# Feed-forward down projections with seven block products per pair of chunks instead of eight

## Chip, cores, metric

One core of one Trainium2 chip runs the whole program. Times are microseconds of device time, the median of 3 runs. TensorE (PE) multiplies, VectorE (DVE), ScalarE (ACT) and GpSimd (POOL) work element by element, SyncE (SP) issues most of the loads. All data are fp32.

## What is computed

The reference is a model of three blocks on 256 tokens of width 1024. Two layers of the first kind each have two feed-forwards around a mixer (a state-space scan, then neighbourhood attention) and end in a gated side input; a third layer of another kind follows, with three attention branches and a squared-ReLU MLP. What the change touches are the four feed-forwards:

```
D_MODEL = 1024; SEQ = 256; D_FF = 2816
def swiglu(x, w_gu, w_down):
    g, u = jnp.split(x @ w_gu, 2, axis=-1)
    return (jax.nn.silu(g) * u) @ w_down
for i in range(DEPTH):                      # 2 layers
    h = h + 0.5 * swiglu(rmsnorm(h, ffn1_norm[i]), ffn1_w_gu[i], ffn1_w_down[i])
    ...                                     # the mixer
    h = h + 0.5 * swiglu(rmsnorm(h, ffn2_norm[i]), ffn2_w_gu[i], ffn2_w_down[i])
    ...                                     # the gated side input
```

A down projection multiplies 256 x 2816 by 2816 x 1024.

## The kernel before

**Products.** Every fp32 product is made of three matmuls in the fp32r type: both operands are split into a rounded part ("hi") and the residue ("lo"), and hi*hi, hi*lo and lo*hi are added up in PSUM. For weights the hi part is a ScalarE copy from `raw` to `whi`, the lo part a VectorE subtraction `wlo = raw - whi` (the function `ahead` of each engine, the operations themselves in the helpers `copy`, L1412, and `tt`, L1967).

**The stream of weight tiles.** `plan_of` (L156) lists all 284 tiles of the program in their order, each up to 128 x 2048 elements, 1 MB. SyncE loads them in this order into four slots (`NRAW`), each load waiting until the slot's earlier tile is split. ScalarE and VectorE split tiles into three slots (`NSPL`). `take(label)` on each of the two marks the place where a tile is used, and first splits ahead: the tile two after it. ScalarE's split waits for the load and until TensorE has released the tile three before it. TensorE waits for both parts (`take`, L574) and signals `w_rel` when it has used them. So the order of all work on an engine is the order in which its program calls `take` and the steps between.

**A feed-forward** (`ffn` in each engine's program). The up stage has 11 steps `c`, each with two tiles, 48 matmuls of 512 columns: the first 256 columns are gate, the second 256 are up. ScalarE makes the SiLU into `ftmp`, VectorE the product into `fa`, 128 tokens x 256 features for each of two token halves `t`. One step later, TensorE transposes it (`turn_a`) into PSUM bank 4 or 5, and `high_a` (ScalarE) and `low_a` (VectorE) split it into `aThi` and `aTlo`: 22 chunks of 128 features x 256 tokens, the stationary operand of the down projection.

The down stage (`down`, L724) goes over column halves `c` of 512 columns and in each over 6 tiles of four chunks (the last one of two). For each chunk and token half, three matmuls of 512 columns add to a PSUM bank: banks 6 and 7 for the first half of the columns, 2 and 3 for the second. That is 22 x 2 x 2 x 3 = 264 matmuls. VectorE adds 0.5 x bank to `h` (`residual`), the next stage's transposes (`turn`), squares and splits (`early_quarters`, `late_quarters`) are placed between the tiles of the second half and behind it.

**GpSimd** takes the inverse square roots of the norms (one-column powers, `rstds`), some sums in the state-space mixer (gate<-gate), the bias sums of the neighbourhood attention (bm<-tb,cst) and two residues in the third layer. It is idle in feed-forwards but for the roots. The bias table `tb` is loaded by `table` in SyncE's program.

Of the kernel before, what the change touches and what calls it, by code (L numbers as in the profile page):

```python
# [18 lines left out]
TILE = 2048  # L19

# [23 lines left out]
def constants():  # L44
# [30 lines left out]
    "a_weigh": "exps", "v_outputs": "yev yg yTlo", "a_outputs": "yThi ysq",  # L75
# [69 lines left out]
class Plan:  # L145


    def __init__(self):
        self.tiles, self.index = [], {}

    def add(self, label, pieces, a, b):
        self.index[label] = len(self.tiles)
        self.tiles.append((pieces, a, b))


def plan_of(dr):  # L156
    p = Plan()

    def ffn(i, up, down, extra=None):
# [64 lines left out]
PREP = (8, 16, 24)  # L224
HALVES = 2 * len(PREP) + 2
# [129 lines left out]
def programs(dr, mem, banks, plan, ev):  # L355
# [11 lines left out]
    pool_tiles = set()  # L367

    def wview(name, n):
        _, a, b = plan.tiles[n]  # L370
        slots = NRAW if name == "raw" else NSPL
        return mem[name][:, n % slots, 0:a * b].rearrange("p (a b) -> p a b", a=a)

    def wflat(name, n, slots):
        _, a, b = plan.tiles[n]
        return mem[name][:, n % slots, 0:a * b]
# [117 lines left out]
    def sync(S):  # L494
# [3 lines left out]
        def load(n):  # L498
            pieces, a, b = plan.tiles[n]
            slot = wflat("raw", n, NRAW).rearrange("p (a b) -> p a b", a=a)  # L500
            if n >= NRAW:
                last = (n - NRAW,) if n - NRAW > 1 else (n - NRAW, 3)
                S.wait_ge(*at("w_hi", *last))
                S.wait_ge(*at("w_lo" if n - NRAW not in pool_tiles else "w_lo_p", *last))
            c = 0
            for src in pieces:
                wd = src.shape[2]
                e.dma_start(slot[:, :, c:c + wd], src).then_inc(*sig(f"d_w{n % NRAW}", n, by=16))
# [8 lines left out]
        def table():  # L517
            rp = dr["rpb"]
            S.wait_ge(*at("h", 4, 1, 1))
# [23 lines left out]
        for n in range(2, len(plan.tiles)):  # L543
# [4 lines left out]
            if n == tile["down", 2, 0, 0]:  # L548
                pos(1)
# [10 lines left out]
    def tensor(T):  # L560
# [13 lines left out]
        def take(*label):  # L574
# [5 lines left out]
            T.wait_ge(*at("w_lo_p" if n in pool_tiles else "w_lo", n))  # L580
# [115 lines left out]
        def closing_block(labels, bs, xhi, xlo, first, between=None):  # L696
# [6 lines left out]
            for t in range(2):  # L703
                for i, (label, hi, lo, kk) in enumerate(held):
                    nk = hi.shape[1]
                    for k in range(nk):
# [4 lines left out]
                        if between and t and i == 0 and k == 1:  # L711
                            between()
# [11 lines left out]
        def down(name, xhi, xlo, tiles, r, turn_last):  # L724

            for c in range(2):
                bs = ACC[c]
                clear(*bs)
                for y in range(tiles - 2):
# [3 lines left out]
                    if y == 0:  # L733
                        if c == 0:
                            turn_last()
                        elif r < 10:
                            turn(r, 0, 0)
                            turn(r, 1, 0)
# [2074 lines left out]
```

## Time and profile before

| | |
|---|---|
| median of 3 runs | 1678.13 us (1677.65 to 1678.68) |
| span of the profiled execution | 1676.1 us |
| TensorE busy | 1664.8 us (99%) |
| VectorE busy | 1068.0 us (64%) |
| ScalarE busy | 898.6 us (54%) |
| GpSimd busy | 86.1 us (5%) |
| weight residues wlo on VectorE | 284, 622.4 us |
| weight hi parts on ScalarE | 284, 518.2 us |
| bytes moved | 300.58 MB, mean 179 GB/s |

The profiled execution's span is 2.0 us under the median of the runs: the span is counted from the first to the last instruction. Busy time of TensorE is the union of its matmuls, whose ends are modelled; the time that one matmul costs is read from start to start. The rows that the prediction rests on stand below.

### The profile page before, as it was taken

The page shows a single profiled execution, that of the slowest core. Times are in us where ns is not written, and L with a number is a line of the kernel's source. Part 1 is how long each engine was busy: PE and PEld are TensorE (multiplying, and loading weights), DVE is VectorE, ACT ScalarE, POOL GpSimd, SP SyncE. Part 2 cuts the span into 40 slices and gives each one's busy share as a digit, 9 for nine tenths or more (in the row PEclk, how much of TensorE's full clock was granted, in tenths as well). Part 3 has the DMA queues.
Part 4 walks back from the last instruction along what each step waited for, and adds up shares of the span by engine and source line. Part 5 has one row for each costly group of instructions (what it writes and reads, how often), then busy time and mean ns, then how long its engine had stood idle before and what let it go on. Part 6 is the DMA issues. An engine that isn't in the chain of part 4 may idle for free.

```text
span 1676.1 us, 23021 instructions
## 1 busy us (share of the span) xinstructions
PE 1664.8 (99%) x9366; PEld 1426.7 (85%) x9366; DVE 1068.0 (64%) x1364; ACT 898.6 (54%) x1279; POOL 86.1 (5%) x79
## 2 busy tenths in 40 slices
PE   8999999999999999999999999999999999999998
PEld 6888899999788888888888778888889999988886
DVE  5554678999965545755457766555655577766643
ACT  5443566777864444744346665444553556564532
POOL 0000000000100000000007500000000000000000
PEclk9999999999999999999999999999999999999999
DMA  9655567666466554686555336655565533465551
GB/s 306 192 178 184 158 191 208 179 196 209 156 200 198 187 188 165 188 242 209 181 175 195 119 101 214 185 180 188 180 197 153 174 103 126 152 211 178 176 192 60
DMA packets 243978, 300.58 MB, mean 179 GB/s; under 512 B 9248, under 2 KB 175520, under 8 KB 243872
## 3 DMA queue, kind: packets, MB, share of 16 engines
q1 hardware_dynamic: 238224, 289.25, 54.5%
q10 hardware_dynamic: 5648, 9.85, 2.2%
q8 instruction: 75, 1.23, 0.3%
q14 instruction: 31, 0.25, 0.0%
HBM read 297.96 MB, written 1.11 MB: 178 GB/s over the span
## 4 chain that ended last, share of the span: by engine, by line
PE 99%; DVE 1%; DMA 0%; ACT 0%; ACTq 0%; DVEq 0%; issue 0%
PE bank L564 95%; PE bank L567 4%; DMA h<-in_x 0%; DVE wlo L1967 0%; DVE hTlo L1970 0%; DVE xn L1970 0%; DVE h L1970 0%; ACT hThi L1412 0%; DVE xn L2019 0%; DVEq L2740 0%; ACT xn L1409 0%; ACTq L1924 0%; ACTq L1923 0%; ACT L1920 0%; ACTq L2740 0%
## 5 line engine op out<-in xcount | busy, mean ns | idle before, releaser
L1967 DVE TENSOR_TENSOR wlo<-raw,whi 128x2048 fp32r<-128x2048 f32 (+2 forms) x284 | 622.4, 2195 | 326.5 <-ACT whi L1412 326.5
L1412 ACT ACTIVATE whi<-raw 128x2048 fp32r<-128x2048 f32 (+2 forms) x284 | 518.2, 1832 | 244.8 <-PE bank L564 240.9
L564 PE MATMUL bank<-whi,hThi 128*128 128x512 f32 x1056 | 420.7, 398 | 0.0
L564 PE MATMUL bank<-wlo,hThi 128*128 128x512 f32 x1056 | 412.3, 390 | 0.3 <-DVE wlo L1967 0.3
L564 PE MATMUL bank<-whi,hTlo 128*128 128x512 f32 x1056 | 396.8, 391 | 0.0
L564 PE MATMUL bank<-hThi,whi 128*128 128x256 f32 x888 | 253.3, 285 | 0.0
L564 PE MATMUL bank<-hThi,wlo 128*128 128x256 f32 x888 | 251.2, 283 | 0.0
L564 PE MATMUL bank<-hTlo,whi 128*128 128x256 f32 x888 | 251.2, 283 | 0.0
L564 PEld LDWEIGHTS bank<-whi,hThi 128*128 128x128 f32 x1056 | 198.6, 188 | 44.3 <-issue 6.0
L564 PEld LDWEIGHTS bank<-whi,hTlo 128*128 128x128 f32 x1056 | 198.5, 188 | 42.6 <-DVE hTlo L1970 0.3
L564 PEld LDWEIGHTS bank<-wlo,hThi 128*128 128x128 f32 x1056 | 198.8, 188 | 40.5 <-DVE wlo L1967 1.8
L564 PEld LDWEIGHTS bank<-hThi,whi 128*128 128x128 f32 x888 | 169.5, 191 | 3.6 <-issue 3.1
L564 PEld LDWEIGHTS bank<-hThi,wlo 128*128 128x128 f32 x888 | 169.5, 191 | 0.2
L564 PEld LDWEIGHTS bank<-hTlo,whi 128*128 128x128 f32 x888 | 169.5, 191 | 0.2
L564 PE MATMUL bank<-whi,aThi 128*128 128x512 f32 x352 | 137.8, 391 | 0.0
L564 PE MATMUL bank<-whi,aTlo 128*128 128x512 f32 x352 | 137.1, 389 | 0.0
L564 PE MATMUL bank<-wlo,aThi 128*128 128x512 f32 x352 | 137.0, 389 | 0.0
L1412 ACT ACTIVATE aThi<-bank 128x512 fp32r<-128x512 f32 x44 | 26.3, 598 | 155.1 <-PE bank L567 155.1
L1409 ACT ACTIVATE ftmp<-bank,st 128x256 f32<-128x256 f32 x88 | 41.5, 475 | 105.6 <-PE bank L564 105.5
L2564 POOL TENSOR_TENSOR st<-st,cst 128x1 f32<-128x1 f32 (+2 forms) x35 | 36.5, 1057 | 1147.4 <-DVE st L1992 1075.2
L1967 DVE TENSOR_TENSOR aTlo<-bank,aThi 128x512 fp32r<-128x512 f32 x44 | 30.4, 691 | 80.8 <-ACT aThi L1412 80.8
L564 PEld LDWEIGHTS bank<-whi,aTlo 128*128 128x128 f32 x352 | 66.1, 188 | 13.8
(222 smaller groups left out, 1883.4 us busy)
## 6 DMA issues: line engine op xcount, KB each, us to landing
raw<-in_ffn_w_gu SPq DMA_DIRECT2D x172, 512.0 KB, 4.9
raw<-in_ffn_w_down SPq DMA_DIRECT2D x40, 1024.0 KB, 5.0
raw<-in_w_in SPq DMA_DIRECT2D x30, 1024.0 KB, 5.2
raw<-in_ssd_w_in SPq DMA_DIRECT2D x16, 1024.0 KB, 5.6
raw<-in_ssd_w_in SPq DMA_DIRECT2D x32, 512.0 KB, 5.5
raw<-in_w_up SPq DMA_DIRECT2D x16, 1024.0 KB, 5.4
raw<-in_w_down SPq DMA_DIRECT2D x16, 1024.0 KB, 5.0
raw<-in_na_w_qkv SPq DMA_DIRECT2D x12, 1024.0 KB, 5.2
```

Of the source, the lines that this page charges most:

```text
L564: return T.e.matmul(out, lhsT, rhs, start=start, stop=stop, skip_group_check=skip)
L567: return T.e.transpose(out, in_, ident)
L1409: return e.activation(out, in_, func, **kw)
L1412: return e.activation(out, in_, ACT.Identity, **kw)
L1967: return e.tensor_tensor(out, a, b, op)
L2564: return e.tensor_tensor(out, a, b, op)
```

## The change

For 14 of the 22 chunks, in 7 pairs, the 2 x 2 block matrix of activations (two token halves x two chunks) is multiplied with the 2 x 2 block matrix of weights (two chunks x two column halves) with seven block products in place of eight, after Strassen and Winograd. Write A11, A21 for the two token halves of the pair's first chunk, A12, A22 for those of the second, and B11, B12 (first chunk), B21, B22 (second chunk) for the column halves of the weights.

- **Weights.** A `paired` tile is a load of 2 chunks x 1024 columns, in the order B12, B11, B22, B21. Its last 1536 columns are split. A `mixed` tile is not loaded: it is the four sums B11+B12, B12+B22, B11+B12+B22, B11+B12+B22+B21, made by GpSimd (1024 columns in one operation, then 512) and VectorE (the last 512) in one of three buffers `ts0` to `ts2`, and then split like any tile, 2048 columns. `ts1` and `ts2` lie where the normalised input of the up stage was, `ts0` on the buffers of the differences.
- **Activations.** ScalarE copies the transposes of the first 7 steps also into `araw`; GpSimd makes the differences `dsum`, in operations of 256, 128 and 128 columns (`differences`); ScalarE and VectorE split them (`high_d`, `low_d`) one step later. In place of A21 split directly at the place of the second token half, `aThi` holds there what the seven products need.
- **Order of the down stage** (`mixed_down` in three engines' programs): a tile of four chunks of the first column half (chunks 14 to 17), the last transposes, pair 0, pair 1, a tile of two chunks of the second half, pairs 2 to 6, then the last four chunks of the first half and the last six of the second. A pair is 9 matmuls with the paired tile and 12 with the mixed one.
- **Merge.** The seven products go to all eight banks; products shared by several blocks are added at the end by six VectorE operations, one ScalarE copy and two GpSimd sums of 512 columns (`merged`), before the residuals.
- `table` waits for the last mixed tile of the third feed-forward and is issued before a tile of the attention; the GpSimd path for weight residues (`pool_tiles`, empty) goes; in GpSimd's program the roots, pair sums and merges are put in the order of the stages.

The core of the diff:

```diff
+PAIRS = 7
...
+REST = {(0, 0): (14, 4), (0, 1): (18, 4), (1, 0): (14, 2), (1, 1): (16, 4), (1, 2): (20, 2)}
...
-        for c in range(2):
-            for y in range(6):
-                nk = min(4, 22 - 4 * y)
-                p.add(("down", i, c, y), [wsrc(down, 4 * y, nk, c * 512, 512)], nk, 512)
+        rest(0, 0)
+        for j in range(PAIRS):
+            p.add(("paired", i, j), [wsrc(down, 2 * j, 2, 512, 512), wsrc(down, 2 * j, 2, 0, 512)], 2, 1024)
+            p.add(("mixed", i, j), None, 4, 512)
+            if j == 1:
+                rest(1, 0)
+        rest(0, 1)
+        rest(1, 1)
+        rest(1, 2)
...
 SyncE, load(n)
                 S.wait_ge(*at("w_hi", *last))
-                S.wait_ge(*at("w_lo" if n - NRAW not in pool_tiles else "w_lo_p", *last))
+                S.wait_ge(*at("w_lo", *last))
+                if labels[m][0] == "paired":
+                    S.wait_ge(*at("tsum", *labels[m][1:]))
...
 SyncE, table
-            S.wait_ge(*at("h", 4, 1, 1))
+            S.wait_ge(*at("w_rel", "mixed", 2, PAIRS - 1))
...
-            if n == tile["up", 2, 0, 0] + 8:
+            if n == tile["qkv", NA_CHUNKS[1], 0]:
                 table()
...
 TensorE
+            def seven(j):
+                first, final = j == 0, j == PAIRS - 1
+                hi, lo = take("paired", i, j)
+                T.wait_ge(*at("aTlo", i, j))
+                T.wait_ge(*at("dTlo", i, j))
+                three_products(0, block_of(2 * j, 0), hi[:, 0, 512:1024], lo[:, 0, 512:1024], first, final)
+                three_products(2, difference(j, 2), hi[:, 1, 0:512], lo[:, 1, 0:512], first, False)
+                three_products(6, block_of(2 * j + 1, 0), hi[:, 1, 512:1024], lo[:, 1, 512:1024], False, False).then_inc(
+                    *sig("w_rel", "paired", i, j))
+                hi, lo = take("mixed", i, j)
+                if first:
+                    clear(4)
+                three_products(4, difference(j, 0), hi[:, 0, :], lo[:, 0, :], first, final)
+                three_products(5, block_of(2 * j, 1), hi[:, 1, :], lo[:, 1, :], first, final)
+                three_products(1, difference(j, 1), hi[:, 2, :], lo[:, 2, :], first, final)
+                three_products(7, block_of(2 * j + 1, 1), hi[:, 3, :], lo[:, 3, :], False, False).then_inc(*sig("w_rel", "mixed", i, j))
...
+            clear(6, 7)
+            rest(0, 0, (6, 7), (True, True))
+            turn_last()
+            clear(0, 1, 2, 3, 5)
+            for j in range(PAIRS):
+                seven(j)
+                if j == 1:
+                    rest(1, 0, (2, 3), (False, True))
...
+            closing_block([("down", i, 0, 1)], (6, 7), aThi, aTlo, REST[0, 1][0])
+            residual_in(r, 0, (6, 7))
+            held, k0 = [], REST[1, 1][0]
+            for y in (1, 2):
+                hi, lo = take("down", i, 1, y)
+                held += [(hi[:, k, :], lo[:, k, :], y) for k in range(REST[1, y][1])]
...
 ScalarE, high_a
+                if c >= 2:
+                    A.wait_ge(*at("dsum", i, c - 2))
+                copy(mem["araw"][:, c % 2, :], b).then_inc(*sig("araw", i, c))
+                copy(aThi[:, 2 * c, 0:P], b[:, 0:P])
+                copy(aThi[:, 2 * c + 1, :], b[:, 256:512]).then_inc(*sig("aThi", i, c))
+
+            def high_d(c):
+
+                A.wait_ge(*at("dsum", i, c))
+                d = mem["dsum"][:, c % 2, :]
+                copy(aThi[:, 2 * c, P:256], d[:, 0:P])
+                copy(flat(mem["dThi"][:, c, :, :]), d[:, P:512]).then_inc(*sig("dThi", i, c))
...
 VectorE, ahead
+                if labels[n][0] == "paired":
+                    w, o = mem["raw"][:, plan.raw_of[n] % NRAW, :], mem[f"ts{labels[n][2] % 3}"][:, :]
+                    V.wait_ge(*at("tsecond", *labels[n][1:]))
+                    tt(o[:, 1536:2048], o[:, 1024:1536], w[:, 1536:2048], ALU.add).then_inc(*sig("tsum", *labels[n][1:]))
                 V.wait_ge(*at("w_hi", n))
...
 VectorE
+            def low_d(c):
+
+                V.wait_ge(*at("dThi", i, c))
+                d = mem["dsum"][:, c % 2, :]
+                tt(aTlo[:, 2 * c, P:256], d[:, 0:P], f(aThi[:, 2 * c, P:256]), ALU.subtract)
+                tt(flat(dTlo(c)), d[:, P:512], f(flat(mem["dThi"][:, c, :, :])), ALU.subtract).then_inc(*sig("dTlo", i, c))
+
+            def merged():
+
+                um, wm = flat(mem["ftmp"][:, :, :]), flat(fa[:, :, :])
+                V.wait_ge(*at("root", i))
+                stt(h[:, 0, chunk(0)], banks[0], 0.5, h[:, 0, chunk(0)], ALU.mult, ALU.add).then_inc(*sig("h11", i))
+                V.wait_ge(*at("w_rel", "mixed", i, PAIRS - 1))
+                stt(um, banks[1], 0.5, um, ALU.mult, ALU.subtract).then_inc(*sig("um", i))
+                stt(h[:, 0, chunk(1)], banks[4], 0.5, h[:, 0, chunk(1)], ALU.mult, ALU.add).then_inc(*sig("h12p", i))
+                V.wait_ge(*at("um", i))
+                stt(wm, banks[5], 0.5, um, ALU.mult, ALU.add).then_inc(*sig("wm", i))
+                stt(h[:, 1, chunk(1)], banks[4], 0.5, h[:, 1, chunk(1)], ALU.mult, ALU.add).then_inc(*sig("h22p", i))
+                V.wait_ge(*at("wm", i))
+                tt(h[:, 1, chunk(0)], h[:, 1, chunk(0)], wm, ALU.subtract).then_inc(*sig("h21", i))
+
+            def mixed_down(r):
+                take("down", i, 0, 0)
+                low_a(10)
+                for j in range(PAIRS):
+                    take("paired", i, j)
+                    take("mixed", i, j)
+                    if j == 1:
+                        take("down", i, 1, 0)
+                merged()
+                take("down", i, 0, 1)
+                V.wait_ge(*at("h21", i))
+                for t in range(2):
+                    residual(r, t, 0, half(("down", i, 0, 1), t), 6 + t, 0.5)
+                take("down", i, 1, 1)
+                early_quarters(r)
+                V.wait_ge(*at("h22", i))
...
 GpSimd
+        def sums(i, j):
+
+            n = tile["paired", i, j]
+            w, o = mem["raw"][:, plan.raw_of[n] % NRAW, :], mem[f"ts{j % 3}"][:, :]
+            halves = lambda x: x.rearrange("p (x c) -> p x c", x=2)
+            G.wait_ge(*landed(n))
+            if j >= 3:
+                G.wait_ge(*at("w_lo", tile["mixed", i, j - 3]))
+            elif j:
+                G.wait_ge(*at("w_rel", "up", i, 10, 1))
+            else:
+                G.wait_ge(*at("dTlo", i, PAIRS - 1))
+            tt(halves(o[:, 0:1024]), halves(w[:, 512:1536]), w[:, 0:512].unsqueeze(1).to_broadcast([P, 2, 512]), ALU.add).then_inc(*sig("tfirst", i, j))
+            G.wait_ge(*at("tfirst", i, j))
+            tt(o[:, 1024:1536], o[:, 0:512], w[:, 1024:1536], ALU.add).then_inc(*sig("tsecond", i, j))
+
+        def ffn(i, extra=None):
+            for c in range(PAIRS):
+                differences(i, c)
+                if c == 2 and extra is not None:
+                    ple_rstd(extra)
+            for j in range(PAIRS):
+                sums(i, j)
+            G.wait_ge(*at("h12p", i))
+            tt(h[:, 0, chunk(1)], h[:, 0, chunk(1)], flat(mem["ftmp"][:, :, :]), ALU.add).then_inc(*sig("h12", i))
+            G.wait_ge(*at("wm", i))
+            G.wait_ge(*at("h22p", i))
+            tt(h[:, 1, chunk(1)], h[:, 1, chunk(1)], flat(mem["fa"][:, :, :]), ALU.add).then_inc(*sig("h22", i))
```

## Rows read from the trace of the kernel before

**Rows 1.** The page, part 1: engine, busy us, share of the span, instructions.

```profile
PE 1664.8 (99%) x9366; PEld 1426.7 (85%) x9366; DVE 1068.0 (64%) x1364; ACT 898.6 (54%) x1279; POOL 86.1 (5%) x79
```

**Rows 2.** Waits of TensorE: total us, times, longest.

```profile
PE bank L567 <- DMA h<-in_x: 2.8, 2, 2.5
PE bank L564 <- DVE fa L2532: 1.2, 1, 1.2
PE bank L564 <- DVE wlo L1967: 0.3, 1, 0.3
```

**Rows 3.** Order of time on TensorE: start us, us of the instruction, operation.

```profile
136.94 0.39 PE L564 MATMUL bank<-whi,aThi 128*128 128x512 f32 x1
...
139.66 0.39 PE L564 MATMUL bank<-whi,aThi 128*128 128x512 f32 x1
```

**Rows 4.** Groups by shape, ScalarE and VectorE: busy us, mean ns, idle before.

```profile
L1412 ACT ACTIVATE whi<-raw 128x2048 fp32r<-128x2048 f32 x262 | 500.1, 1913 | 208.4 <-PE bank L564 204.5 <-DMA cum<-ct 3.2 <-DMA raw<-in_ffn_w_gu 0.7
L1412 ACT ACTIVATE whi<-raw 128x1024 fp32r<-128x1024 f32 x12 | 12.7, 1057 | 28.2 <-PE bank L564 28.2
L1967 DVE TENSOR_TENSOR wlo<-raw,whi 128x1024 fp32r<-128x1024 f32 x12 | 14.7, 1223 | 18.8 <-ACT whi L1412 18.8
```

**Rows 5.** The page, part 6: KB of one load, us from issue to landing.

```profile
raw<-in_ffn_w_down SPq DMA_DIRECT2D x40, 1024.0 KB, 5.0
```

**Rows 6.** Order of time on VectorE, back-to-back operations.

```profile
416.62 0.68 DVE L1967 TENSOR_TENSOR EW<-Er,cst 128x512 f32<-128x512 f32 x1
417.22 0.68 DVE L1967 TENSOR_TENSOR Er<-Er,later 128x512 f32<-128x512 f32 x1
...
449.73 2.28 DVE L1967 TENSOR_TENSOR wlo<-raw,whi 128x2048 fp32r<-128x2048 f32 x1
451.93 3.54 DVE L1967 TENSOR_TENSOR EW<-EW,bank 128x1024 f32<-128x1024 f32 x4
```

**Rows 7.** Order of time on GpSimd; x12 is a run of twelve.

```profile
453.31 1.30 POOL L2564 TENSOR_TENSOR gate<-gate 128x512 f32<-128x512 f32 x1 [9.14 <-DVE EW L1967]
458.58 3.21 POOL L2564 TENSOR_TENSOR gate<-gate 128x512 f32<-128x512 f32 x1 [3.97 <-ACT gate L1409]
...
895.95 7.29 POOL L2564 TENSOR_TENSOR bm<-tb,cst 128x256 f32<-128x256 f32 x8
...
906.39 14.15 POOL L2564 TENSOR_TENSOR bm<-tb,cst 128x256 f32<-128x256 f32 x12
...
1027.98 0.54 POOL L2564 TENSOR_TENSOR st<-st,cst 128x1 f32<-128x1 f32 x1 [22.14 <-DVE st L2105]
1028.70 2.52 POOL L2564 TENSOR_TENSOR st<-st,cst 128x1 f32<-128x1 f32 x1 [0.18 <-DVE st L2105]
...
1375.95 3.14 POOL L2564 TENSOR_TENSOR oS<-oT,oS 128x1024 fp32r<-128x1024 f32 x1 [156.57 <-ACT oS L1412]
```

**Rows 8.** Order of time on VectorE, residues beside the GpSimd operations of rows 7.

```profile
458.35 2.28 DVE L1967 TENSOR_TENSOR wlo<-raw,whi 128x2048 fp32r<-128x2048 f32 x1
...
896.68 2.75 DVE L1967 TENSOR_TENSOR wlo<-raw,whi 128x2048 fp32r<-128x2048 f32 x1
...
907.15 5.46 DVE L1967 TENSOR_TENSOR wlo<-raw,whi 128x2048 fp32r<-128x2048 f32 x2
...
915.04 2.85 DVE L1967 TENSOR_TENSOR wlo<-raw,whi 128x2048 fp32r<-128x2048 f32 x1
...
1028.55 2.28 DVE L1967 TENSOR_TENSOR wlo<-raw,whi 128x2048 fp32r<-128x2048 f32 x1
...
1374.56 2.29 DVE L1967 TENSOR_TENSOR wlo<-raw,whi 128x2048 fp32r<-128x2048 f32 x1 [1.06 <-ACT whi L1412]
```

**Rows 9.** Order of time on VectorE, two residual additions in a feed-forward.

```profile
170.39 1.28 DVE L1970 SCALAR_TENSOR_TENSOR h<-bank,h 128x512 f32<-128x512 f32 x2
```

**Rows 10.** Stretches of an up stage: busy us of each engine, clock, DMA.

```profile
30.00:100.00 70.00, 70.00 (x322) 57.90 (x321) 37.78 (x33) 32.72 (x31) 0.00 (x0) 1.00 0.65 204
```

**Rows 11.** The same view at the opening; PEclk 1.00 is full speed.

```profile
5.00:10.00 5.00, 2.39 (x10) 1.63 (x10) 1.61 (x5) 2.26 (x8) 0.00 (x0) 0.80 1.02 350
```

More of the change, by code:

```diff
@@ L542, in sync @@
         e.dma_start(cst[:, 130:NCST], dr["cst"][:, 130:NCST]).then_inc(*sig("d_c2", by=16))
-        for n in range(2, len(plan.tiles)):
+        for n in plan.raws[2:]:
             if n == tile["yout", 7] + 5:
                 pos(0)
-            if n == tile["up", 2, 0, 0] + 8:
+            if n == tile["qkv", NA_CHUNKS[1], 0]:
                 table()
-            if n == tile["down", 2, 0, 0]:
                 pos(1)
@@ L579, in take @@
             T.wait_ge(*at("w_hi", n))
[L580 removed]
+            T.wait_ge(*at("w_lo", n))
             return wview("whi", n), wview("wlo", n)
@@ L735, in down @@
                             turn_last()
[L736 to L740 removed]
+                closing_block([name + (c, tiles - 2), name + (c, tiles - 1)], bs, xhi, xlo, 4 * (tiles - 2))
                 residual_in(r, c, bs)
@@ new lines, in mixed_down @@
+            def mixed_down(r):
+                take("down", i, 0, 0)
+                low_a(10)
+                for j in range(PAIRS):
+                    take("paired", i, j)
+                    take("mixed", i, j)
+                    if j == 1:
+                        take("down", i, 1, 0)
+                merged()
+                take("down", i, 0, 1)
+                V.wait_ge(*at("h21", i))
+                for t in range(2):
+                    residual(r, t, 0, half(("down", i, 0, 1), t), 6 + t, 0.5)
+                take("down", i, 1, 1)
+                early_quarters(r)
+                V.wait_ge(*at("h22", i))
+                for t in range(2):
+                    residual(r, t, 1, half(("down", i, 1, 2), t), 2 + t, 0.5)
+                    if r == 1 and t == 0:
+                        low(1, 0, 1)
+                        mean_square(1, 0)
+                if r == 1:
+                    scaled(0)
+                take("down", i, 1, 2)
+                if r == 1:
+                    mean_square(1, 1)
+                    low(1, 1, 1)
+                    scaled(1)
+                else:
+                    late_quarters(r)
@@ L2564, in tt @@
             return e.tensor_tensor(out, a, b, op)
-        def ahead(m):
-            while G.ready < min(m, len(plan.tiles)):
-                n = G.ready
-                G.ready += 1
-                if n in pool_tiles:
-                    G.wait_ge(*at("w_hi", n))
-                    tt(wflat("wlo", n, NSPL), wflat("raw", n, NRAW), f(wflat("whi", n, NSPL)), ALU.subtract).then_inc(*sig("w_lo_p", n))
-        def take(*label):
-            ahead(tile[label] + NSPL)
         def rstds(r):
@@ L2637, in three @@
             for what, n in three_steps():
-                if what == "gate" and n % 2 == 0:
-                    take("gate", n // 2)
-                elif what == "keep" and n in (3, 7):
+                if what == "keep" and n in (3, 7):
                     br = n // 4
```

198 lines of the change are left out of this document (135 added, 63 removed).

## The prediction

> **What bounds the kernel now.** I read the page from its totals downward: TensorE is busy for 1664.8 of 1676.1 us [rows 1]. The modelled ends of the matmuls could make that share look too good, so the second view is who waited for whom: TensorE waited 4.3 us in the whole execution, only 0.3 us of it for a weight split [rows 2]. So nothing but the number of matmuls sets the time, and a microsecond of them removed anywhere is a microsecond of span, as long as the other engines still deliver ahead of TensorE. Third, the order of time on TensorE at the start of a down projection: from 136.94 to 139.66 lie twelve equal steps, 2.72 / 12 = 0.2267 us from start to start; the 0.39 us of one is its latency, which overlaps the next [rows 3].
>
> **What the change removes.** A pair of 128-row chunks against both column halves and both token halves is eight block products of three matmuls, 24; now it is seven, 21. That is 3 x 7 pairs x 4 feed-forwards = 84 matmuls of 512 columns, 84 x 0.2267 = 19.0 us; a down projection goes from 264 matmuls to 243. The weights' bytes stay the same. With nothing else, the time would be 1678.1 - 19.0 = 1659.1 us (the profiled span is 1676.1; what lies around it is the difference to the median of the runs, 2.0 us, and I leave it as it is).
>
> **What it adds, per pair.** ScalarE: splits of 1536 and 2048 columns in place of one of 2048. At 1.91 us for 2048 and 1.06 for 1024 [rows 4] that is 1.5 + 1.9 = 3.4 us, against a pair's TensorE time of 21 x 0.2267 = 4.76 us: hidden. DMA: one 1 MB load per pair, 5.0 us to landing, asked for at least a pair ahead: hidden [rows 5].
>
> VectorE: the residues of 1536 and 2048 columns and one sum of 512. A 2048-column residue holds VectorE for 2.20 us (449.73 to 451.93 [rows 6]), one of 1024 for about 1.14 (its 1.22 [rows 4] less the same overlap), so one of 1536 for about 1.67; a two-input SBUF operation of 512 takes 0.60 to the next (416.62 to 417.22 [rows 6]). Sum 2.20 + 1.67 + 0.60 = 4.47 us, still under 4.76.
>
> GpSimd: a sum of 1024 columns and one of 512. A free 512-column sum takes 1.30 us, some 1.2 of it without its start-up; 1024 columns took 3.14 us, of which the first 0.90 lay under a VectorE residue, so 2.24 free (1375.95 in [rows 7], 1374.56 in [rows 8]). Sum 2.24 + 1.2 = 3.44 us, also under 4.76.
>
> **Where I see the cost: the two do not run side by side.** [Rows 7] and [rows 8] have to be laid over each other. The 512-column GpSimd sum takes 1.30 us at 453.31 and 3.21 us at 458.58. In the second case VectorE's residue wlo<-raw,whi runs from 458.35 to 460.63, and the sum ends at 461.79, 1.16 us later: it did its whole work afterwards. A one-column power takes 0.54 us free and 2.52 us at 1028.70; the residue beside it ends at 1030.83, the power 0.39 us after that. The reverse also happens: the residue at 896.68 took 2.75 us instead of 2.29, with GpSimd in a run of eight bias sums, 7.29 us with that residue inside. Taking its 2.20 out leaves 0.64 for one. Twelve of them from 906.39 lie beside three residues, two from 907.15 and one at 915.04: 12 x 0.64 + 3 x 2.20 = 14.3, and the row has 14.15. By contrast the sum at 453.31, beside VectorE operations with one operand in PSUM (EW<-EW,bank from 451.93 [rows 6]), was not delayed. So in this kernel VectorE with two SBUF inputs and GpSimd exclude each other for a whole instruction, in turns.
>
> The Trainium skill states this as a rule that speaks against the change (SBUF — State Buffer, section "SBUF: two separate sides"): the port pair that both engines share is an exclusive lock held for the instruction, and a VectorE operation with two SBUF inputs takes it against a GpSimd operation that reads SBUF. By that rule, the trace agrees, the sum comes out as below; without it, as in rival A.
>
> All the new work is of that kind: residues, sum, GpSimd sums. A pair needs 4.47 + 3.44 = 7.9 us of a resource for which TensorE leaves it 4.76.
>
> **How much of that reaches the end.** Let time 0 be where TensorE finishes the last up tile; before it GpSimd can do only the first pair's sums, since the other two sum buffers lie on the up stage's inputs. The last mixed tile can be multiplied once its residue is done, which needs, after time 0: on VectorE seven mixed residues, 7 x 2.20 = 15.4, six paired ones, 6 x 1.67 = 10.0, six sums, 3.6, and the residue of the two-chunk tile, 1.14, together 30.2; on GpSimd six pairs' sums, 6 x 3.44 = 20.6. Sum 50.8 us. TensorE would be there after 24 matmuls, 5.4, the last transposes, 0.4 (an estimate: under two matmuls' worth for four narrow ones), six pairs, 28.6, nine matmuls, 2.0, and the two-chunk tile, 2.7: 39.1 us. It is late by 11.7 us. Stepping through in turns I find no long time when both are idle, and VectorE never waits for ScalarE, since a pair that takes 7.9 us leaves its 3.4 free. Four feed-forwards: 46.8 us.
>
> Bounds: if start-up that queued instructions hide takes 0.2 us off each GpSimd operation (12) and 0.1 off each VectorE one (20), the sum is 46.4 and the lateness 7.3 (four times, 29); if each of some 32 turns costs 0.1 us and the 1024-column sum takes the whole 3.14 us of its row, it is 50.8 + 3.2 + 5.4 = 59.4, 20.3 us late (four times, 81). I take 11.7, since the run of 14.15 us fits turns without a price.
>
> **The end of the down projection.** After it starts the last mixed tile (2.7) TensorE has a four-chunk tile (5.4) before it needs the residue of the last two-chunk tile. From the same moment VectorE has two residues of 2.20, six merges of 512 columns at about 0.64 (two h sums take 1.28 [rows 9]) and that residue, 1.14: 9.4 us, and 1.2 more if a GpSimd sum of the merge is in front. TensorE waits 1.3 to 2.5 us, less what VectorE is ahead; I take 1.5, four times 6 us, between 0 and 12. The residuals that follow are due 2.0 us later and take 1.3: hidden.
>
> **At nothing.** In the up stage GpSimd's differences (512 columns a chunk in three operations, some 1.5 us), the extra ScalarE copies (about 1.3 us) and the extra small residues (0.6 us) lie in a block of 48 matmuls, 10.9 us, of which VectorE is busy for little over half (37.78 of 70 us [rows 10]). A residue behind a difference waits 0.7 us and is due half a block, 5.4 us, later. Without that cover it would be 0.7 us x 28 = 20 us. The bias table's load waits for the third feed-forward's last mixed tile, 15 us before the stage ends; the loads queued behind it on SP are for tiles later than the closing ones, and its users start in the attention. GpSimd's new order puts the norm roots where their inputs come anyway.
>
> **Sum.** 1678.1 - 19.0 + 46.8 + 6.0 = 1711.9, so 1712 us.
>
> **The rivals.**
> A, the other side, faster: the exclusion is not what these rows show, for instance because sums with a repeated operand read differently, and GpSimd's sums slip beside the residues. Then VectorE needs 4.47 and GpSimd 3.44 of 4.76 us, each in time, and the merge remains: 1659.1 + 6 = 1665 us. The change gains once the lateness is under (19.0 - 6.0) / 4 = 3.25 us, so once 8.4 of the 20.6 us of GpSimd's sums slip. Against it: every overlap that I found, in both directions, has the delay. Chance 0.10.
> B, half: 4 to 8 us of the sums slip, lateness about 6 us: 1659.1 + 24 + 6 = 1689 us. For it: no row shows how much of an instruction's own start-up lies outside the exclusion, and queued ones may hide it. Chance 0.14.
> C, worse: turns have a price, or the wide sum takes 3.14: up to 1659.1 + 81 + 6 = 1746 us. A second way there: TensorE idling 3 us in 8 could lower its clock. The profile shows 0.80 between 5 and 10 us [rows 11], after the sparse opening, and full clock ever after; with TensorE working 60% of the time I expect full clock. Chance 0.12.
> D, no effect: gain and loss cancel, lateness near 3.25 us. 0.02.
>
> **How the numbers follow.** Forecast 0.62 (1698 to 1730), B 0.14, C 0.12, A 0.10, D 0.02. A measurement here tells about 0.2%, 3.4 us, from no change. Faster: A and a little of B, 0.11; same: D, 0.02; slower: the rest, 0.87. Range 1684 to 1736: it takes in most of B and the lower half of C and leaves A out.
>
> **What would show it.** In the order of time of a down projection: VectorE and GpSimd working in turns, GpSimd's 1024-column sums at 2.2 us free and up to 4.5 with a residue in front, 2048-column residues at up to 4.4 instead of 2.29. TensorE waiting for wlo, some 45 us in total, in mixed and paired tiles from the second pair on, and 1 to 2 us for the last wlo of each feed-forward. No gaps in up stages, clock full. The prediction is wrong if residues beside GpSimd sums stay at 2.29 us and the sums at 2.2 and 1.3 (then A); if they are undisturbed and TensorE waits anyway, the waits name another place.

## The result and the profile after

| | before | changed |
|---|---|---|
| median | 1677.89 us (1677.38 to 1678.68, 4 runs) | 1724.85 us (1720.34 to 1726.17, 4 runs) |
| ratio to before | | 1.0274, 95% interval 1.0260 to 1.0289 |
| span of the profiled execution | 1676.1 us | 1718.5 us |

The change makes the kernel 2.7% slower. The forecast was slower, 1712 us, range 1684 to 1736. The profiled execution of the changed kernel is the lowest of its four runs (1720.34); the others have spans of 1722.2 to 1724.4, so the median lies some 4.5 us above what the trace below can account for.

The page of the changed kernel, the parts that answer to [rows 1]: busy us, share and instructions of each engine, then the engines' shares of the chain of work that ended last.

```profile
PE 1663.9 (97%) x9282; PEld 1413.2 (82%) x9282; DVE 1229.2 (72%) x1528; ACT 971.0 (57%) x1423; POOL 290.1 (17%) x227
...
PE 87%; DVE 11%; ACT 1%; DMA 0%; issue 0%; DVEq 0%; ACTq 0%
```

84 matmuls are gone (9366 to 9282), the span is longer. The chain that ended last, second line, now has VectorE for 11%. The waits of TensorE, answering to [rows 2] (total us, times, longest):

```profile
PE bank L602 <- DVE wlo L2103: 26.3, 17, 2.3
PE bank L602 <- issue: 11.5, 10, 1.5
PE bank L602 <- ACT whi L1520: 6.1, 6, 2.0
```

The residues that TensorE waited 0.3 us for now cost it 26.3 us. The next two lines name something else, but in the down stages each of these waits, too, ends 0.10 us after the end of a weight residue on VectorE, so they are waits for the same tiles. But for 0.6 us of the opening and the first up stage, all of it lies in the down stages. From the first to the last matmul of each down projection it was 61.5, 61.0, 61.0 and 61.0 us before and 73.8, 71.2, 71.3 and 71.3 us after, together 43.0 us more; the three stretches between them and the one behind the last changed by less than 0.1 us, the opening by 0.4. The second of them as one stretch, before and then after (length, busy us of PE, PEld, DVE, ACT, POOL, clock, DMA share, GB/s):

```profile
604.60:665.60 61.00, 61.00 (x277) 50.62 (x276) 28.02 (x24) 24.28 (x26) 0.00 (x0) 1.00 0.53 182
```

```profile
616.50:687.70 71.20, 60.42 (x256) 46.91 (x255) 63.55 (x43) 35.96 (x34) 35.43 (x14) 0.98 0.51 170
```

VectorE goes from 28 busy us of 61 to 63.6 of 71.2, much of it not work but waiting inside the instruction. That is seen when its order of time is laid beside GpSimd's, as [rows 7] and [rows 8] were. The first down projection, VectorE:

```profile
145.34 2.85 DVE L2103 TENSOR_TENSOR wlo<-raw,whi 128x1536 fp32r<-128x1536 f32 x1
148.11 4.49 DVE L2103 TENSOR_TENSOR wlo<-ts,whi 128x2048 fp32r<-128x2048 f32 x1
152.52 2.29 DVE L2103 TENSOR_TENSOR wlo<-raw,whi 128x1024 fp32r<-128x1024 f32 x1
154.74 2.88 DVE L2103 TENSOR_TENSOR ts<-ts,raw 128x512 f32<-128x512 f32 x1
...
178.66 1.75 DVE L2103 TENSOR_TENSOR wlo<-raw,whi 128x1536 fp32r<-128x1536 f32 x1
...
185.60 2.29 DVE L2103 TENSOR_TENSOR wlo<-ts,whi 128x2048 fp32r<-128x2048 f32 x1 [0.32 <-ACT whi L1520]
```

and GpSimd in the same stretch:

```profile
136.80 2.41 POOL L2746 TENSOR_TENSOR ts<-raw 128x1024 f32<-128x1024 f32 x1 [14.60 <-PE bank L602]
...
144.95 1.62 POOL L2746 TENSOR_TENSOR ts<-ts,raw 128x512 f32<-128x512 f32 x1
146.54 3.91 POOL L2746 TENSOR_TENSOR ts<-raw 128x1024 f32<-128x1024 f32 x1
150.53 3.21 POOL L2746 TENSOR_TENSOR ts<-ts,raw 128x512 f32<-128x512 f32 x1
153.70 3.37 POOL L2746 TENSOR_TENSOR ts<-raw 128x1024 f32<-128x1024 f32 x1
...
173.30 2.69 POOL L2746 TENSOR_TENSOR ts<-ts,raw 128x512 f32<-128x512 f32 x1
```

Read the ends. GpSimd ends at 146.57, 150.45, 153.74; in between VectorE gets its turn and ends at 148.19 and 152.60. A residue of 2048 columns that takes 2.29 us free takes 4.49, one of 1024 columns 2.29 (free 1.22), a sum of 512 columns 2.88 (free 0.69). After 176 us GpSimd has finished, and VectorE's rows are back at 1.75 and 2.29 us.

### The profile page after: what moved, and what is told of

It is laid out like the page before. It is cut to its first block, busy times and chain, and to the rows that moved or that the text cites. A ratio compares the mean times of both kernels' runs of the same rounds, so it can differ in the third digit from the quotient of the medians.

```text
span 1718.5 us, 23453 instructions
## 1 busy us (share of the span) xinstructions
PE 1663.9 (97%) x9282; PEld 1413.2 (82%) x9282; DVE 1229.2 (72%) x1528; ACT 971.0 (57%) x1423; POOL 290.1 (17%) x227
## 4 chain that ended last, share of the span: by engine, by line
PE 87%; DVE 11%; ACT 1%; DMA 0%; issue 0%; DVEq 0%; ACTq 0%
PE bank L602 83%; DVE wlo L2103 8%; PE bank L605 4%; DVE ts L2103 1%; ACT whi L1520 0%; DVE h L2106 0%; DMA prm<-in_prm 0%; DVE h L2103 0%; DVE aTlo L2103 0%; ACT aThi L1520 0%; DVE ftmp L2106 0%; DVE fa L2106 0%; ACT hThi L1520 0%; DVE rTlo L2106 0%; DVE hTlo L2106 0%
## 5 line engine op out<-in xcount | busy, mean ns | idle before, releaser
L2103 DVE TENSOR_TENSOR wlo<-raw,whi 128x2048 fp32r<-128x2048 f32 (+2 forms) x284 | 641.2, 2263 | 208.0 <-ACT whi L1520 207.6
L1520 ACT ACTIVATE whi<-raw 128x2048 fp32r<-128x2048 f32 (+2 forms) x284 | 507.3, 1792 | 164.7 <-PE bank L602 161.2
L602 PE MATMUL bank<-whi,aThi 128*128 128x512 f32 x240 | 98.2, 409 | 26.6 <-issue 11.5
L2746 POOL TENSOR_TENSOR ts<-raw 128x1024 f32<-128x1024 f32 x28 | 79.9, 2853 | 158.5 <-DMA raw<-in_ffn_w_down 75.1
L602 PE MATMUL bank<-whi,aTlo 128*128 128x512 f32 x240 | 95.5, 398 | 0.0
L602 PE MATMUL bank<-wlo,aThi 128*128 128x512 f32 x240 | 95.3, 397 | 0.0
L1520 ACT ACTIVATE whi<-ts 128x2048 fp32r<-128x2048 f32 x28 | 53.7, 1918 | 64.1 <-DVE ts L2103 61.6
L2103 DVE TENSOR_TENSOR wlo<-ts,whi 128x2048 fp32r<-128x2048 f32 x28 | 81.8, 2920 | 7.8 <-ACT whi L1520 7.8
```

Source lines behind the costliest of these rows:

```text
L602: return T.e.matmul(out, lhsT, rhs, start=start, stop=stop, skip_group_check=skip)
L1520: return e.activation(out, in_, ACT.Identity, **kw)
L2103: return e.tensor_tensor(out, a, b, op)
L2746: return e.tensor_tensor(out, a, b, op)
```

## The experiments

Times are medians, ratios against the kernel before run on the same chip in the same call.

**GpSimd writes, but reads nothing.** Weight sums left out, constant fills of the same columns in their place.

```diff
-            tt(halves(o[:, 0:1024]), halves(w[:, 512:1536]), w[:, 0:512].unsqueeze(1).to_broadcast([P, 2, 512]), ALU.add).then_inc(*sig("tfirst", i, j))
+            e.memset(o[:, 0:1024], 0.5).then_inc(*sig("tfirst", i, j))
...
-            tt(o[:, 1024:1536], o[:, 0:512], w[:, 1024:1536], ALU.add).then_inc(*sig("tsecond", i, j))
+            e.memset(o[:, 1024:1536], 0.5).then_inc(*sig("tsecond", i, j))
```

> Leaves out the weight sums of GpSimd: in their place it fills the same 1024 and 512 columns with a constant, in the same place of its program and behind the same semaphores, so it writes but reads nothing. Theory P (VectorE with two SBUF inputs and GpSimd reading SBUF exclude each other): GpSimd takes no turns from VectorE any more, the 2048-column residues of mixed tiles fall from 2.92 us mean to 2.29, the 1536-column ones from 2.70 to 1.76, TensorE waits only at the merge (4 x 2.4 us) and at full clock: 1659 + 10 = 1669 us, 1664 to 1675. Rival W (they exclude each other whatever GpSimd does): fills of perhaps a third of the sums' time still block, 1685 to 1700. Rival V (VectorE is bound by its own added work, not by turns): its work is unchanged, 1718 to 1728.

Measured 1675.44 us (1671.86 to 1677.56), ratio 0.9984 (0.9975 to 0.9993): VectorE's own added work is all still there, and the time is 49 us below the changed kernel's. It is 0.4 us over the range expected, and the granted clock goes with that: the five runs at 0.998 took 1671.9 to 1674.6 us, the five at 0.994 to 0.996 took 1676.3 to 1677.6. Rival V (VectorE bound by its own work) is out. The groups by shape (busy us, mean ns, idle before), first the changed kernel's:

```profile
L2103 DVE TENSOR_TENSOR wlo<-ts,whi 128x2048 fp32r<-128x2048 f32 x28 | 81.8, 2920 | 7.8 <-ACT whi L1520 7.8
L2103 DVE TENSOR_TENSOR wlo<-raw,whi 128x1536 fp32r<-128x1536 f32 x28 | 75.5, 2695 | 0.4
```

then this one's:

```profile
L2103 DVE TENSOR_TENSOR wlo<-ts,whi 128x2048 fp32r<-128x2048 f32 x28 | 64.2, 2293 | 17.3 <-ACT whi L1520 17.3
L2103 DVE TENSOR_TENSOR wlo<-raw,whi 128x1536 fp32r<-128x1536 f32 x28 | 49.1, 1755 | 1.9 <-ACT whi L1520 1.2
```

Both residues are back at their free duration. The fills are shorter than the sums (0.96 and 0.53 us), so this alone does not say that they don't exclude VectorE. Two rows where they overlap do, GpSimd and VectorE of this kernel:

```profile
157.57 0.96 POOL L2841 MEMSET ts<- 128x1024 f32 x1 [3.59 <-DVE wlo L2103]
158.59 0.53 POOL L2843 MEMSET ts<- 128x512 f32 x1
...
157.97 1.75 DVE L2103 TENSOR_TENSOR wlo<-raw,whi 128x1536 fp32r<-128x1536 f32 x1
```

Neither is prolonged. The exclusion needs a GpSimd operation that reads; rival W is out.

**The last sum back on GpSimd.**

```diff
 VectorE, ahead
-                    tt(o[:, 1536:2048], o[:, 1024:1536], w[:, 1536:2048], ALU.add).then_inc(*sig("tsum", *labels[n][1:]))
 GpSimd, sums
+            G.wait_ge(*at("tsecond", i, j))
+            tt(o[:, 1536:2048], o[:, 1024:1536], w[:, 1536:2048], ALU.add).then_inc(*sig("tsum", i, j))
```

> Undoes one part: the last weight sum (512 columns) of each pair goes back to GpSimd. Theory P: GpSimd gets 1.24 us more a pair and VectorE 0.60 less, the sum grows by 0.64 x 6 = 3.8 us a feed-forward: 1724.9 + 15 = 1740 us, 1732 to 1748. Rival V: VectorE is relieved of 0.60 x 6 x 4 = 14 us: 1711 us. Rival L (GpSimd works ahead and only the hand-overs count): about as now, 1720 to 1730.

Measured 1738.03 us (1736.95 to 1739.47), ratio 1.0358 (1.0342 to 1.0373): 13 us slower than the changed kernel. Work taken off the busier engine made it slower, because the other one holds the shared resource twice as long for it. Of the three readings on record only the sum over both engines has that sign. It is not the whole of it: the last mixed residue now ends 56.3 us after the first down matmul, 4.9 later than in the changed kernel where 3.8 was expected, since VectorE stands idle three times for 3.1 us in each stage, waiting for GpSimd's sums and ScalarE's copy of them; part of that comes back at the end of the stage.

**The residue in front of the merge.**

```diff
-                merged()
                 take("down", i, 0, 1)
+                merged()
                 V.wait_ge(*at("h21", i))
```

> VectorE's residue of the last two-chunk tile is placed before the six merges instead of behind them. The gap of 2.7 us from start to start at the last block of each feed-forward (2.4 us lost) goes; the merges come 1.1 us later and the transposes of the next stage, due 2.0 us into the block, may wait about 0.5 us: 1724.9 - 4 x 1.9 = 1717 us, 1713 to 1721. If the gap is not the residue's but the merges' (banks or h), no change, 1722 to 1727.

Measured 1709.28 us (1708.70 to 1709.83), ratio 1.0187 (1.0170 to 1.0204). That is 15.6 us below the changed kernel, twice what was expected. The gap of 2.7 us from start to start is gone and nothing takes its place in three of four stages (68.8 us against 71.2). The first takes 69.8 against 73.8: there a stretch at half clock (granted clock 0.5, some 1.4 us lost) lay in the closing block, and it is gone as well. The stages together give 11.4 us, and 0.3 lies in the opening. Most of the rest comes from the profiled runs: the changed kernel's lies 4.5 us under its median, this one's 0.6. So the merge order was worth 2.4 us a stage, not 1.5, and in the first stage the half clock on top of it.

**All sums on VectorE**, each in front of the residue of its paired tile.

```diff
 VectorE, ahead, of a paired tile
-                    V.wait_ge(*at("tsecond", *labels[n][1:]))
+                    V.wait_ge(*landed(n))
+                    ...  # the two sums of GpSimd's sums(i, j), then the third
 GpSimd, ffn
-            for j in range(PAIRS):
-                sums(i, j)
```

> All three weight sums (1024, 512, 512 columns) on VectorE, none on GpSimd. Theory P: a 512-column sum costs the shared resource 0.60 us on VectorE and 1.2 on GpSimd, so a pair needs 2.20 + 1.67 + 1.14 + 0.60 + 0.60 = 6.2 us of it instead of 7.9; after time 0 that is 15.4 + 10.0 + 1.1 + 6 x 2.34 = 40.6 us against TensorE's 39.1: 1.5 us late, with some 0.3 us a pair of waiting for whi about 3. Time 1659 + 4 x (3 + 2.4) = 1681 us, 1673 to 1692, the half-clock windows mostly gone. Rival V (VectorE's own time bounds): 1.74 us more per pair on VectorE on top of today's lateness, 6 x 1.74 x 4 = 42 us more: 1766 us. Rival L (the hand-over GpSimd, VectorE, ScalarE, VectorE is what costs): one hand-over less, 1700 to 1715.

Measured 1713.65 us (1712.50 to 1714.85), ratio 1.0212 (1.0197 to 1.0227). Faster than the changed kernel by 11 us, but 33 us off the expectation. Rival V is out again, but the time lies in the range of rival L, so this run alone does not decide between L and the sum. The trace has free durations for the sums and for the paired and mixed residues, and each pair takes 6.86 us on VectorE, from start to start 1.25 and 1.34 for the sums, 1.75 for the paired residue, a wait of 0.31 for ScalarE's whi and 2.21. Lateness had been summed as if VectorE worked from time 0; it stood still for some 3 us before the last aTlo, and the first sum, in line behind it, began 7.3 us after time 0.

**Seven pairs, the same sums ahead.** Sums of pair 1 right after the up stage, of pair 2 before aTlo, of pair j + 1 between the two residues of pair j; four-chunk tiles for the two-chunk ones.

```diff
 VectorE, after the residue of tile n
+                if labels[n][0] == "paired" and 3 <= labels[n][2] + 1 < PAIRS:
+                    vsum(labels[n][1], labels[n][2] + 1)
 VectorE, mixed_down
+                vsum(i, 1)
                 take("down", i, 0, 0)
+                vsum(i, 2)
                 low_a(10)
```

> Seven pairs, sums of pairs 1 to 6 on VectorE but placed ahead: those of pairs 1 and 2 right after the up stage, where VectorE stood idle for 4 us, each further one between the paired and the mixed residue of the pair before; the tiles of two chunks made into tiles of four. If the run with all sums on VectorE missed its forecast because of idle time (4 us at the start and 0.3 us a pair, in order behind waits), this gives it back: VectorE has 15.4 + 10.0 + 2.2 + 6 x 2.5 + 0.6 = 43.2 us, a wait or two about 1, against TensorE's 41.8: 2.4 us late a feed-forward. 1659.1 + 4 x (2.4 + 0.5) = 1671 us, 1666 to 1680. If VectorE's sums cost something else, about 1705 as before less the merge.

Measured 1688.88 us (1688.07 to 1689.11), ratio 1.0062 (1.0048 to 1.0075). 25 us less than with the sums in line, and still 18 us over the expectation. Not all of the 25 is the order of the sums: the tiles of four chunks leave no residue behind the merge, and with it goes a wait of 2.1 us a stage, 8.4 us. TensorE still waits 18.8 us for wlo and 4.8 us for aTlo. Even placed well, 6.4 us of VectorE a pair against 4.76 of TensorE does not fit seven times in a row.

**Five pairs, spread.** Between pairs 1 and 2, 2 and 3, 3 and 4 stands a plain tile of four chunks, 5.4 us of TensorE for 2.2 of VectorE. 60 matmuls fewer than before instead of 84.

```diff
-PAIRS = 7
+PAIRS = 5
+ORDER = [('d', 0, 0), ('p', 0), ('p', 1), ('d', 1, 0), ('p', 2), ('d', 0, 1), ('p', 3), ('d', 1, 1), ('p', 4)]
```

> Five pairs (10 of 22 chunks), the six remaining four-chunk tiles spread: one first, three between pairs, two last; sums of pairs 1 to 4 on VectorE, those of pair 0 on GpSimd in the up stage, VectorE's sums placed after the mixed residue before a spread tile. Three matmuls x 5 x 4 = 60 fewer than before: 13.6 us. Theory P: up to the last mixed tile VectorE has 5 x 2.20 + 4 x 1.67 + 3 x 2.20 + 4 x 2.5 = 34.3 us, TensorE 5.4 + 0.4 + 4 x 4.76 + 2.0 + 3 x 5.44 = 43.1: no lateness, and the last tile has no residue behind the merges. 1678.1 - 13.6 + 0 to 4 = 1664.5 to 1669, faster than before. If the pairs cost TensorE something of their own (a bank or start-up effect), 1670 to 1680.

Measured 1674.44 us (1673.65 to 1675.88), ratio 0.9977 (0.9968 to 0.9986): the first that is faster than before with nothing left out. It is still 5 us over the range expected, in the range of the rival that the pairs cost TensorE something of their own; which it is, the last run below decides. The same `ORDER`, with the sums left in GpSimd's `sums` and VectorE's `ahead` as in the changed kernel:

> The same order with five pairs, but the sums as in the changed kernel (1536 columns on GpSimd, the last on VectorE). Theory P: the shared resource is asked for 11.0 + 6.7 + 6.6 + 4 x 0.60 + 4 x 3.44 = 40.5 us up to the last mixed tile, under TensorE's 43.1, so nearly the same time as with the sums on VectorE: 1665 to 1673. Rival L (each hand-over through GpSimd costs about the 2 us a pair of the changed kernel): 1664.5 + 5 x 4 x 2 = 1700 us.

Measured 1675.39 us (1674.26 to 1678.09), ratio 0.9986 (0.9977 to 0.9995). This is the sharpest test of the sum: 40.5 us of demand against 43.1 us of TensorE, and with GpSimd's sums the kernel takes 1.0 us more than with VectorE's. They are as slow as ever (3.02 and 2.20 us in the mean, 2.85 and 2.34 in the changed kernel); there is room for them. Both times are above what was expected, but a price of each hand-over (rival L) would have given 1700 us, and that is out.

**Where the rest waits.** In the five-pair run TensorE waits once in each down stage (in the first also at the transposes of the next stage, 2.1 us from start to start):

```profile
PE bank L607 <- DVE aTlo L2110: 1.2, 1, 1.2
```

I had taken it for a weight residue. The next run, on that reading, put the sums of pair 1 behind the first mixed residue, and in the first feed-forward TensorE's transposes for the next stage two chunks later:

```diff
-                vsum(i, 1)
                 take("down", i, 0, 0)
+                vsum(i, 1)
                 vsum(i, 2)
                 low_a(10)
```

> The five-pair kernel with two orders mended. VectorE does the residue of the first mixed tile before the sums of pair 1, not after them: the one wait of each down stage, 1.58 us from start to start, goes (1.35 x 4 = 5.4 us). In the first feed-forward the transposes that wait for the second half's h come two chunks later: up to 1.9 us. With the five-pair run at 1674.4: 1674.4 - 5.4 - 1 = 1668 us, 1666 to 1671. If VectorE simply runs late at this place, the wait moves to the first paired tile after it: 1672 to 1675.

Measured 1684.53 us (1684.01 to 1685.87), ratio 1.0039 (1.0025 to 1.0053): 10 us worse. The wait grew from 1.6 to 3.0 us from start to start, 5.7 us in the four stages, and in the last three some seven matmuls behind it run at half clock, 1.35 us each time. The later transposes gained nothing: 2.3 us less in the first stage, 2.3 us more behind it. The wait is `clear(4)` in `seven`: the first mixed tile writes bank 4, which the aTlo in line behind two pairs' sums must free. Six pairs with the same order had the same wait and the same half clock in three stages:

```diff
+PAIRS = 6
+ORDER = [('d', 0, 0), ('p', 0), ('p', 1), ('d', 1, 0), ('p', 2), ('p', 3), ('d', 0, 1), ('p', 4), ('d', 1, 1), ('p', 5)]
```

> Six pairs with the same orders: tiles of four, four, two, two, four and four chunks around them. 12 matmuls fewer than with five pairs, 2.7 us. VectorE up to the last mixed tile: 6 x 2.20 + 5 x 1.67 + 2.2 + 2 x 1.14 + 5 x 2.5 + 0.6 = 39.2 us, TensorE 5.4 + 0.4 + 5 x 4.76 + 2.0 + 5.4 + 5.4 = 42.5: by the sum no lateness, but two pairs stand side by side twice, where a pair asks 6.4 us of VectorE against 4.76: up to 1.6 us each not hidden. 1668 - 2.7 = 1665 us if hidden, 1671 if not; I expect 1667.

Measured 1684.23 us (1683.67 to 1685.20), ratio 1.0037 (1.0025 to 1.0050). Then with the sums of pair 1 first again and those of pair 2 out of aTlo's way, five pairs and six (there with pair 3 behind the first two-chunk tile):

```diff
-                            vsum(i, 2)
                             low_a(10)
...
+                if labels[n][0] == "down" and labels[n][2:] == (1, 0):
+                    vsum(labels[n][1], 2)
```

> The first five-pair kernel with one order changed. Its trace says that the one wait of each down stage (1.58 us from start to start) ends with VectorE's aTlo, the residue of the last transposed activations, which frees PSUM bank 4, and not with a weight residue: VectorE makes the sums of pair 2 in front of it. Moving the sums of pair 1 behind the first mixed residue only pushed that aTlo 3.4 us later and cost 10 us. Here the sums of pair 1 stay first and those of pair 2 go behind the residue of the four-chunk tile that follows pair 1. If the bank is the cause: 1674.4 - 4 x 1.35 = 1669 us, 1667 to 1671. If VectorE is simply short of time at the start of the stage, 1673 to 1676.

> Six pairs in the same order, tiles of four, four, two, two, four and four chunks, the last two pairs side by side. Against five pairs 12 matmuls fewer (2.7 us), and a pair more in front of the last mixed tile, where VectorE needs 6.4 us and TensorE 4.76. If bank 4 is the cause of the wait at the start: 1666 to 1670, I expect 1668.

Measured 1673.79 us (1673.13 to 1675.90), ratio 0.9976 (0.9966 to 0.9986), and 1674.84 us (1673.88 to 1675.46), ratio 0.9978 (0.9970 to 0.9987). The wait at bank 4 is gone in both, and waits for wlo stand further on instead, with five pairs one of 1.53 us from start to start 25 us into each stage, with six three of 0.7 to 1.0, so the time is the same. That is over both forecasts, and as far as the times go VectorE could simply be short of time, as the expectation's rival says. But the trace shows the next sums, of pair 3, in front of a residue that was due. The last run moves these too, and in the first feed-forward the early quarters of the next stage behind the second half's first residual addition:

```diff
+SPREAD = {(1, 0): 2, (0, 1): 3, (1, 1): 4}
...
+                if labels[n][0] == "down" and labels[n][2:] in SPREAD:
+                    vsum(labels[n][1], SPREAD[labels[n][2:]])
```

> In the last five-pair kernel bank 4's wait is gone, but a wait of 1.53 us (start to start) for a weight residue stands 25 us into each down stage: VectorE makes the sums of pair 3 (2.6 us) in front of the residue of the spread four-chunk tile. Here the sums of pairs 2, 3 and 4 each go behind the residue of the spread tile that precedes their pair, where TensorE has 5.4 us of work ready. 4 x 1.3 = 5.2 us less; and in the first feed-forward VectorE adds the second half's h before it splits the early quarters, so that the transposes behind it do not wait (2.08 us from start to start there, at most 1.8 us). 1673.8 - 5.2 - 1 = 1667.5 us, 1666 to 1670. If these waits are VectorE's total load and not its order, the wait moves again and the time stays at 1672 to 1675.

Measured 1667.52 us (1666.66 to 1668.02), ratio 0.9935 (0.9922 to 0.9949), faster than both kernels. One down stage of it, and TensorE's waits in the whole run, to be read beside [rows 2]:

```profile
603.40:661.20 57.80, 57.80 (x262) 47.60 (x262) 50.26 (x46) 31.91 (x31) 2.99 (x2) 1.00 0.54 186
```

```profile
PE bank L611 <- DMA h<-in_x: 2.8, 2, 2.2
PE bank L608 <- DVE fa L2740: 1.2, 1, 1.2
PE bank L608 <- DVE wlo L2111: 1.2, 3, 0.6
PE bank L611 <- DVE h L2114: 1.1, 1, 1.1
```

A stage takes 57.7 us from first to last matmul; 61.0 less 15 matmuls of 0.2267 is 57.6. Nothing of the gain is lost there, so pairs have no price of their own on TensorE, and the waits were a matter of order. Of the 13.6 us that 60 matmuls are worth, 10.7 arrive: 1.8 us are lost between the first and the second down stage, where TensorE waits for the second half's h (the last line), and the rest in pieces of under 0.5 us. The changed order of the early quarters took 1.7 us from the end of the first stage and put 0.7 behind it.

## Why the prediction was right, and by how much it was off

- **What bounds the kernel before, and what 84 matmuls are worth:** right. With the sums' reads taken out the stages fall to 59.3 us; less the merge gap of 2.4 that is 56.9, and 61.0 - 21 x 0.2267 is 56.2. The 0.7 us between them lie in some ten steps of 0.24 to 0.32 us from start to start. (The first stage takes 61.8 us, with a half-clock stretch in its closing block.)
- **The exclusion, as the place of the cost:** right, in both directions, and by the runs that vary it alone (fills 49 us faster; the last sum moved to GpSimd 13 us slower, 15 expected).
- **The sum of 50.8 us up to the last mixed residue:** the residue ends at 187.89, the first down matmul starts at 136.49: 51.4 us. The 1024-column sum takes 2.41 us free, against 2.24 from the overlapped row of [rows 7]. Turns have no visible price. That VectorE never waits for ScalarE was wrong: it stands idle for 4.5 us of the 51.4, most of it in the first 7 us, for whi and aThi. It did not matter, since GpSimd worked meanwhile; in the second stage there are only 0.9 us in which neither was busy.
- **The merge, 1.5 us:** too small. The step said 1.3 to 2.5 us "less what VectorE is ahead"; 2.4 us are lost in every stage (2.66 from start to start). VectorE is not ahead, and the case with a GpSimd sum in front holds. VectorE, then GpSimd, in the changed kernel:

```profile
196.32 2.28 DVE L2103 TENSOR_TENSOR wlo<-raw,whi 128x1024 fp32r<-128x1024 f32 x1
...
195.82 1.71 POOL L2746 TENSOR_TENSOR h<-h,fa 128x512 f32<-128x512 f32 x1
```

  The last residue takes 2.28 instead of 1.22 us. This is the term of the sum that was mis-sized.
- **TensorE's clock:** put into rival C at 0.12, and it happens, but it cost little. In the first down projection:

```profile
162.00:165.40 3.40, 3.40 (x10) 2.62 (x9) 3.40 (x3) 1.91 (x1) 2.68 (x1) 0.50 0.81 296
```

  Clock 0.50 is the lower of its two levels, 1.2 GHz, after a stretch with gaps; matmuls start 0.43 us apart instead of 0.2267. Each stage has one such stretch among its pairs, and the first a second one in the closing block. Mean over the kernel 0.993, against 0.998 before. In the profiled runs with few or short gaps (GpSimd reading nothing, and all with five to seven pairs but the two with the 3 us wait) it is 0.998 or 0.999, in those two 0.996 and 0.995.

  Seven matmuls at half clock take 1.4 us more, but among the pairs TensorE only waits that much less for VectorE behind them. The first stage up to the end of its last mixed residue, and from there to its last matmul, in the changed kernel:

```profile
136.50:187.90 51.40, 42.77 (x176) 32.80 (x174) 46.90 (x22) 25.80 (x17) 32.47 (x12) 0.97 0.41 137
187.90:210.30 22.40, 19.81 (x86) 15.66 (x85) 16.21 (x26) 10.60 (x24) 2.97 (x2) 0.92 0.68 188
```

  and with the residue in front of the merge, where this stage has full clock:

```profile
136.20:187.60 51.40, 41.26 (x176) 31.57 (x174) 46.93 (x22) 25.76 (x17) 32.50 (x12) 1.00 0.42 137
187.60:206.00 18.40, 18.06 (x86) 14.46 (x85) 15.26 (x27) 10.64 (x24) 3.00 (x2) 1.00 0.82 229
```

  The first part takes 51.4 us with and without the half clock, and so it does in all eight down stages of these two kernels. In the closing block no wait for a weight follows, and there the 1.4 us are lost, once in the kernel. Nothing in the forecast's sum stood for them. Where TensorE has little to wait for behind it, a stretch costs in full: with six pairs and the 3 us wait the third stage, which has none, takes 60.9 us, the others 62.3 to 62.6.
- Together, a stage from the second on lost 15.0 us (71.2 - 61.0 + 4.8) where the forecast had 13.2: 0.6 of the difference up to the last mixed residue, 0.9 at the merge, the rest in small steps. The first lost 17.1, of its 2.1 more 1.4 by the half clock and 0.5 in a wait for h at the next stage's transposes. That makes 9.3 us. The profiled span is 8.6 us over the forecast's (1718.5 against 1676.1 + 33.8), the median of the runs 4.5 us more than that. What the other three runs lost, no trace shows.
- **At nothing:** right. Up stages, attention with the later table, and the state-space mixer kept their lengths within 0.1 us; the opening varied by 0.4.
- The 45 us of wlo waits that I named came as 26.3 us, with 17.6 us more booked under two other names for the same tiles; 9.1 us of this are the four waits behind the merge, for which I had 1 to 2 us each.

## What to carry to other kernels

Where two engines exclude each other, add their durations as if they were one engine, and compare that sum with the time of the engine that bounds; each one's busy share says nothing. Moving work to the idle engine is then a loss if that engine is slower at it, even when it has the time. And where an engine's queue is in order, a sum of work only gives a lower bound: look at which wait stands at its head, and put deferrable work behind the residue that is due next, where the bounding engine has most work in stock. A stretch at half clock is no loss by itself either: it counts where the engine does not have to wait again behind it.

## What the runs showed of the hardware

- VectorE with two SBUF inputs and GpSimd reading SBUF take turns by whole instructions: 2.29 us becomes up to 4.49, GpSimd's 1.30 up to 3.22. A GpSimd fill, which only writes, runs beside a residue at 0.96 and 0.53 us with no delay on either side.
- For fp32 sums GpSimd needs twice VectorE's time: 2.41 us against 1.22 for 1024 columns, 1.30 against 0.69 for 512.
- VectorE operations with one operand in PSUM do not take part in this: the GpSimd sum at 194.56 us in the merge takes 1.29 us beside two of them, of 0.68 us each, as the one at 453.31 did before ([rows 6], [rows 7]).
- Waits of 1 to 3 us among matmuls, with TensorE otherwise at work, were followed by stretches at half clock of some seven matmuls, one or two in each down stage of the changed kernel and with the last sum on GpSimd. It is not one fixed length of wait: the same 2.7 us behind the merge brought one in one stage of four where GpSimd read nothing, and the waits of 1.6 to 1.9 us with seven pairs ahead brought none. I had expected full clock.
